# Attention by keys and values of each head in place of latent queries and outputs, with the work at three entries in another order

## What is computed

```
q = jnp.einsum('bsr,rhd->bshd', cq, w_uq)
q_lat = jnp.einsum('bshd,hdr->bshr', q, w_uk)
...
_, sel = lax.top_k(score, n_sel)                      # 64 keys per query
kv_sel = jax.vmap(lambda c, i: c[i])(ckv, sel)
att = jnp.einsum('bqhr,bqkr->bqhk', q_lat_b, kv_sel) * (A_HEAD_DIM ** -0.5)
att = att - slopes[None, None, :, None] * dist[:, :, None, :]
p = jax.nn.softmax(jnp.where(valid, att, -jnp.inf), axis=-1)
o_lat = jnp.einsum('bqhk,bqkr->bqhr', p, kv_sel)
return jnp.einsum('bqhr,hrd->bqhd', o_lat, w_uv)
...
return jnp.concatenate([o_a, o_b], axis=-1) @ w_out
```

## Time and profile before

| | us |
|---|---|
| median of 3 runs | 1978.47 |
| lowest and highest | 1975.74, 1982.19 |
| the profiled execution | 1978.86 |
| its span, first to last instruction | 1977.0 |
| TensorE busy | 1948.3 |
| VectorE, ScalarE, GpSimd busy | 1091.0, 845.2, 65.7 |
| mean granted TensorE clock, of full speed | 0.995 |

### The profile page before, as it was taken

One profiled execution on the slowest core, in us unless ns is written; L12 is line 12 of the kernel. 1 busy time (PEld: TensorE's weight loads), 2 busy tenths in 40 slices (PEclk: granted clock), 3 DMA queues, 4 the chain that ended last, 5 costly groups with the idle time before them and its releaser, 6 DMA issues.

```text
span 1977.0 us, 28705 instructions
## 1 busy us (share of the span) xinstructions
PE 1948.3 (99%) x10670; PEld 1661.4 (84%) x10670; DVE 1091.0 (55%) x1235; ACT 845.2 (43%) x944; POOL 65.7 (3%) x95
## 2 busy tenths in 40 slices
PE   9999999999999998999999999899999999999997
PEld 7888888888888887999999988788888888888886
DVE  5555545555445465677756757555545555544455
ACT  4444434444434343555645544344444444443332
POOL 0000000000000001300221100000000000000000
PEclk9999999999999999999999999999999999999999
DMA  8666665666566573755532057466666666556663
GB/s 293 190 189 190 191 182 179 190 200 210 190 204 203 193 244 95 223 180 148 142 98 87 22 186 261 131 189 190 189 182 183 193 197 190 186 169 194 208 197 144
DMA packets 185327, 357.30 MB, mean 181 GB/s; under 512 B 11296, under 2 KB 23584, under 8 KB 184240
## 3 DMA queue, kind: packets, MB, share of 16 engines
q1 hardware_dynamic: 183568, 347.43, 56.8%
q0 software_dynamic: 1696, 8.99, 1.4%
HBM read 354.28 MB, written 2.10 MB: 180 GB/s over the span
## 4 chain that ended last, share of the span: by engine, by line
PE 95%; DVE 3%; issue 1%; ACT 1%; DMA 0%; SPq 0%; POOL 0%; POOLq 0%; ACTq 0%; DVEq 0%
PE acc L370 27%; PE acc L372 27%; PE acc L371 27%; PE acc L393 3%; PE acc L397 3%; PE acc L395 3%; PE tp L727 1%; DVE wlo L358 1%; PE acc L1946 1%; PE tp L1959 0%; ACT whi L351 0%; PE acc L1972 0%; PE tp L448 0%; DMA raw<-in_ffn_w_gate_dram 0%; DVE work L1691 0%
## 5 line engine op out<-in xcount | busy, mean ns | idle before, releaser
L358 DVE TENSOR_TENSOR wlo<-raw,whi 128x1024 fp32r<-128x1024 f32 (+2 forms) x637 | 762.4, 1204 | 785.5 <-ACT whi L351 784.6
L351 ACT ACTIVATE whi<-raw 128x1024 fp32r<-128x1024 f32 (+2 forms) x637 | 656.2, 1039 | 943.4 <-PE acc L372 880.8
L370 PE MATMUL acc<-whi,xT 128*128 128x512 f32 (+2 forms) x1652 | 636.3, 385 | 13.6 <-DVE wlo L358 12.8
L372 PE MATMUL acc<-whi,xT 128*128 128x512 f32 (+2 forms) x1652 | 631.3, 382 | 0.0
L371 PE MATMUL acc<-wlo,xT 128*128 128x512 f32 (+2 forms) x1652 | 630.8, 382 | 0.0
L370 PEld LDWEIGHTS acc<-whi,xT 128*128 128x128 f32 x1652 | 311.6, 189 | 79.4 <-DVE wlo L358 12.8
L372 PEld LDWEIGHTS acc<-whi,xT 128*128 128x128 f32 x1652 | 311.6, 189 | 59.8
L371 PEld LDWEIGHTS acc<-wlo,xT 128*128 128x128 f32 x1652 | 311.8, 189 | 56.7
L370 PE MATMUL acc<-whi,hT 128*128 128x512 f32 x656 | 256.3, 391 | 0.0
L372 PE MATMUL acc<-whi,hT 128*128 128x512 f32 x656 | 255.4, 389 | 0.0
L371 PE MATMUL acc<-wlo,hT 128*128 128x512 f32 x656 | 255.4, 389 | 0.0
(11 more groups left out here) (299 smaller groups left out, 1283.7 us busy)
## 6 DMA issues: line engine op xcount, KB each, us to landing
raw<-in_ffn_w_up_dram SPq DMA_DIRECT2D x176, 512.0 KB, 3.7
raw<-in_ffn_w_down_dram SPq DMA_DIRECT2D x176, 512.0 KB, 4.6
raw<-in_ffn_w_gate_dram SPq DMA_DIRECT2D x175, 512.0 KB, 3.8
raw<-in_w_in_dram SPq DMA_DIRECT2D x48, 512.0 KB, 3.8
raw<-in_w_out_dram SPq DMA_DIRECT2D x32, 512.0 KB, 6.6
raw<-in_w_in_dram SPq DMA_DIRECT2D x32, 260.0 KB, 2.8
raw<-in_w_in_dram SPq DMA_DIRECT2D x16, 456.0 KB, 5.3
raw<-in_w_q_idx_dram SPq DMA_DIRECT2D x8, 512.0 KB, 4.2
```

What stands on the lines that cost most here:

```text
L351: act.activation(hi[:, s, :, 0:w], raw[:, r, :, 0:w], ACT.Copy).then_inc(hi_done, 1)
L358: dve.tensor_tensor(lo[:, s, :, 0:w], raw[:, r, :, 0:w], hi[:, s, :, 0:w].bitcast(F32), ALU.subtract).then_inc(lo_done, 1)
L370: pe.matmul(o, hi, w_hi[:, s, k, 0:width], start=first and k == 0, stop=False)
L372: ins = pe.matmul(o, lo, w_hi[:, s, k, 0:width], start=False, stop=last and k == UNIT_KT - 1)
```

## The change

The arithmetic of the attention is bracketed in another way. Before, `q_lat = q w_uk` was multiplied with the latents, and the probabilities with the latents and then with `w_uv`. Now `kT`, the keys of each head, is `w_uk` by the latents (per head 2 calls of 256 columns), and a logit is one product of `qT` and `kT`. `vatt`, the values of each head, is the latents by `w_uv` (8 calls of 512 columns for all heads), and a head's output is 3 calls of 128 columns. `w_uk` is laid out on the host with the latent first. `wuv` is loaded once the last score product is done (before: after `qlatT`), to another place. The logits of query tile 1 come first. ScalarE copies `vatt` around the first exponentials; copies, squares and sums of the delta rule stand elsewhere on ScalarE and VectorE; `nkcdT` stands behind the second part of the softmax; the two groups of transposes of L2142 now stand behind units 2 and 3 of the output projection.

At both entries the splits of units 9 and 10 stand ahead of the copies of (2, 1) and (3, 0), and the transposes of (3, 0) and (3, 1) on TensorE each stand one unit earlier. In the first chunk of feed-forward 1 gate and up units alternate for k = 0 and 1, and the later pieces of `x` are loaded behind units 1, 3, 5, 7.

The diff, without allocations and steps that only follow:

```diff
+        FIRST = [(0, 0), (1, 0), (0, 1), (1, 1)] + [(c, k) for c in range(2) for k in range(2, KU)]
+        FIRST_X = {1: 0, 3: 1, 5: 2, 7: 3}
...
             half_unit(7, 1)
+            tile_to_xT_pe(pe, e, 3, 0)
             for half in range(2):
                 half_unit(8, half)
-            tile_to_xT_pe(pe, e, 3, 0)
-            for half in range(2):
-                half_unit(9, half)
             tile_to_xT_pe(pe, e, 3, 1)
-            for v in range(10, 2 * KU):
+            for v in range(9, 2 * KU):
                 for half in range(2):
                     half_unit(v, half)
...
             split_hi(act, p, 0, 8)
+            split_hi(act, p, 0, 9)
             tile_to_xT_act(act, e, 2, 1)
+            split_hi(act, p, 0, 10)
             tile_to_xT_act(act, e, 3, 0)
-            split_hi(act, p, 0, 9)
             tile_to_xT_act(act, e, 3, 1)
-            split_hi(act, p, 0, 10)
...
             norm_tile(dve, e - 1, 3, 0)
             split_lo(dve, p, 0, 8)
-            tile_to_xT_dve(dve, e, 2, 1)
             norm_tile(dve, e - 1, 3, 1)
             split_lo(dve, p, 0, 9)
+            tile_to_xT_dve(dve, e, 2, 1)
+            split_lo(dve, p, 0, 10)
             tile_to_xT_dve(dve, e, 3, 0)
             tile_to_xT_dve(dve, e, 3, 1)
-            split_lo(dve, p, 0, 10)
...
+            for v, (c, k) in enumerate((FIRST, ENTRY)[f]):
+                if f == 0 and v == 0:
+                    load_first(sp, gate_v)
+                else:
                     load_unit(sp, GU[f], 0, v, (gate_v, up_v)[c][:, 2 * k:2 * k + 2, 0:BANK])
+                if f == 0 and v in FIRST_X:
+                    load_x(FIRST_X[v])
...
             pool.tensor_copy(ndist[:], ndist_i[:]).then_inc(sem("ndist"), 1)
+            pool.wait_ge(sem("score_ps"), SCORE_ITEMS)
+            pool.dma_start(wuv[:], w_uv[0].rearrange("h (t r) d -> r h t d", r=P)).then_inc(sem("wuv"), 16)
...
-            for h in range(AH):
-                act.wait_ge(sem("qlat_ps"), h + 1)
-                act.activation(qlatT[:, :, h, :], qlat_bank(h), ACT.Copy).then_inc(sem("qlat"), 1)
+            for pair in range(AH // 2):
+                act.wait_ge(sem("kT_ps"), pair + 1)
+                act.activation(kT[:, 2 * pair:2 * pair + 2, :], kT_bank(pair), ACT.Copy).then_inc(sem("kT"), 1)
             split_hi(act, WO, 0, LEAD)
...
+            def values(t):
+                act.wait_ge(sem("vatt_ps"), t + 1)
+                act.activation(vatt[:, t], all_heads((acc1, acc0)[t]), ACT.Copy).then_inc(sem("vatt"), 1)
+            values(0)
+            exps(0)
+            values(1)
             for b in range(2):
                 four("vnew0", b + 1, b, vnew0, acc1)
-            exps(0)
+            exps(1)
             for b in range(2):
                 four("state", b + 1, b, state, acc1)
-            exps(1)
             act.wait_ge(sem("o0_ps"), 1)
             act.activation(o_first[:], all_heads(acc0), ACT.Copy).then_inc(sem("o_out"), 1)
+            exps(2)
             for b in range(2):
                 four("vnew1", b + 1, b, vnew1, acc1)
-            exps(2)
+            act.wait_ge(sem("o_out"), 1)
+            act.activation(o_squares[:, 0], o_first[:], ACT.Square).then_inc(sem("o_sq"), 1)
             act.wait_ge(sem("pT_ps"), 1)
             act.activation(pT0[:, :, 0:P], tp[:, 0:2].rearrange("p b (h q) -> p (b h) q", h=4), ACT.Copy)\
...
+                oT_hi(h)
+                if h == 5:
                     act.wait_ge(sem("o_sum"), 2)
                     act.activation(o_squares[:, 1], o_second[:], ACT.Square).then_inc(sem("o_sq"), 1)
-            oT_hi(AH - 1)
...
             for q in range(2):
+                split_hi(act, WO, 0, 3 + q)
                 act.wait_ge(sem("yT_ps"), q + 1)
                 act.activation(xT[:, AH + 4 * q:AH + 4 * q + 4, 0, :], yT_banks(q), ACT.Copy)\
                    .then_inc(sem("y_hi"), 1)
...
             logits(1, range(AH // 2))
+            select(1)
+            logits(1, range(AH // 2, AH))
             for b in range(2):
                 dve.wait_ge(sem("nkcd_ps"), b + 1)
                 dve.tensor_scalar(nkcdT[:, 4 * b:4 * b + 4, :], heads4(acc0[:, b]), -1.0, None, ALU.mult)\
                    .then_inc(sem("nkcd"), 1)
-            select(1)
-            logits(1, range(AH // 2, AH))
             normalise(0)
...
             z_times_o(0, o_first[:])
+            o_mean_square(0)
             dve.wait_ge(sem("o_out"), 2)
...
                 dve.wait_ge(sem("pT_ps"), i + 1)
                 dve.tensor_copy(pT0[:, SOFTMAX[i][1], P:S], heads4(pT_bank(i, 0))).then_inc(sem(f"pT_part{i}"), 1)
+            for h in range(4):
+                oT_lo(h)
             dve.wait_ge(sem("o_out"), 3)
             dve.wait_ge(sem("o_sum"), 1)
             dve.tensor_tensor(o_second[:], o_second[:], o_state[:], ALU.add).then_inc(sem("o_sum"), 1)
-            o_mean_square(0)
-            oT_lo(0)
+            for h in range(4, AH):
+                oT_lo(h)
+            y_tile(0)
             dve.wait_ge(sem("o_sum"), 2)
-            oT_lo(1)
             o_mean_square(1)
-            oT_lo(2)
             dve.wait_ge(sem("o_sq"), 2)
             z_times_o(1, o_second[:])
-            oT_lo(3)
-            y_tile(0)
-            oT_lo(4)
             y_tile(1)
-            for h in range(5, AH):
-                oT_lo(h)
...
             for q in range(2):
+                split_lo(dve, WO, 0, 3 + q)
                 dve.wait_ge(sem("y_hi"), q + 1)
...
-            for h in range(AH):
-                if h < 4:
-                    pe.wait_ge(sem("relu"), SCORE_ITEMS - 3 + h)
-                else:
-                    pe.wait_ge(sem("qlat"), h - 3)
-                for r in range(RT):
-                    ins = pe.matmul(qlat_bank(h)[:, r, :], wuk[:, h, r * P:r * P + P], qT[:, h, :],
-                                    start=True, stop=True)
-                ins.then_inc(sem("qlat_ps"), 1)
-            for t in range(T):
+            for pair in range(AH // 2):
+                for j in range(2):
+                    for r in range(RT):
+                        ins = pe.matmul(kT_bank(pair)[:, j, :], wuk[:, r, 2 * pair + j, :], ckvT[:, r, :],
+                                        start=r == 0, stop=r == RT - 1)
+                ins.then_inc(sem("kT_ps"), 1)
+            pe.wait_ge(sem("relu"), SCORE_ITEMS)
+            for t in (1, 0):
                 n = (t + 1) * P
                 for h in range(AH):
-                    pe.wait_ge(sem("qlat"), h + 1 if t == 0 else AH)
-                    for r in range(RT):
-                        ins = pe.matmul((att_first, att_second)[t](h)[:, 0:n], qlatT[:, r, h, t * P:t * P + P],
-                                        ckvT[:, r, 0:n], start=r == 0, stop=r == RT - 1)
+                    pe.wait_ge(sem("kT"), h // 2 + 1)
+                    ins = pe.matmul((att_first, att_second)[t](h)[:, 0:n], qT[:, h, t * P:t * P + P], kT[:, h, 0:n],
+                                    start=True, stop=True)
                     if h % (4, 2)[t] == (3, 1)[t]:
                         ins.then_inc(sem("att_ps"), 1)
+            pe.wait_ge(sem("wuv"), 16)
+            for t in range(T):
+                if t == 1:
+                    pe.wait_ge(sem("att_z"), AH)
+                for b in range(2):
+                    for r in range(RT):
+                        ins = pe.matmul((acc1, acc0)[t][:, b], ckvT[:, r, t * P:t * P + P], wuv[:, 4 * b:4 * b + 4, r, :],
+                                        start=r == 0, stop=r == RT - 1)
+                ins.then_inc(sem("vatt_ps"), 1)
...
             pT_transposes(2)
-            pe.wait_ge(sem("pT_part1"), 2)
-            pe.wait_ge(sem("wuv"), 16)
-            def o_head(h):
-                pe.wait_ge(sem("olat"), h + 1)
-                if h == 0:
-                    pe.wait_ge(sem("o_out"), 2)
+            pe.wait_ge(sem("o_out"), 2)
+            for h in range(AH):
+                if h % 4 == 0:
+                    pe.wait_ge(sem(f"pT_part{h // 4 + 1}"), 2)
                 wait(pe, sem("oT_lo"), h - 3)
-                for r in range(RT):
-                    ins = pe.matmul(o_bank(h), wuv[:, h, r, :], olatT[:, r, h, :], start=r == 0, stop=r == RT - 1)
+                pe.matmul(o_bank(h)[:, 0:P], vatt[:, 0, h], pT0[:, h, 0:P], start=True, stop=True)
+                pe.matmul(o_bank(h)[:, P:S], vatt[:, 0, h], pT0[:, h, P:S], start=True, stop=False)
+                ins = pe.matmul(o_bank(h)[:, P:S], vatt[:, 1, h], pT1[:, h, :], start=False, stop=True)
                 ins.then_inc(sem("oT_ps"), 1)
...
-            pe.wait_ge(sem("o_out"), 3)
-            for h in range(AH):
...
-                    pe.matmul(bank[:, r, 0:P], ckv[:, 0, rc], pT0[:, h, 0:P], start=True, stop=True)
-                    pe.matmul(bank[:, r, P:S], ckv[:, 0, rc], pT0[:, h, P:S], start=True, stop=False)
-                    ins = pe.matmul(bank[:, r, P:S], ckv[:, 1, rc], pT1[:, h, :], start=False, stop=True)
```

(8 more changed lines are left out.)

105 lines of the change are left out of this document (40 added, 65 removed).

## The result

| | before | after |
|---|---|---|
| median, us | 1978.66 (4 runs) | 1951.19 (4 runs) |
| lowest and highest | 1975.74, 1982.19 | 1950.07, 1951.48 |
| the profiled execution | 1978.86 | 1951.33 |
| its span | 1977.0 | 1949.5 |
| ratio of the medians, 95% interval | | 0.9859, 0.9842 to 0.9876 |

What follows compares the result with a forecast made beforehand. It took TensorE's own products to bound the kernel, busy 1948.3 of 1977.0 us. Entries 18.2, start 0.7 and attention 9.5 summed to 28.4 us, taken from 1978.86: 1950.5 us, range 1946 to 1957.

Runs made afterwards that it cites:

- entries_only: The kernel before with only the entries' new order, on all three engines at both entries; attention and first chunk as before: 1961.64 us, ratio 0.9918.
- values_late_2: The kernel after, with `wuv` asked for only when the last `kT` is done, behind GpSimd's masking of the scores: 1952.77 us.
- values_late: The kernel after, with `wuv` asked for only when the last `kT` is done, ahead of GpSimd's masking of the scores: 1956.63 us.
- attention_only: The kernel before with all hunks of the change but those of the entries and the first chunk: 1971.07 us, ratio 0.9967.
- both_chains: The kernel after, with ScalarE's copies ahead of non-urgent exponentials, VectorE's `nkcdT` and transposed-probability copies earlier, splits of output projection units 3 to 5 earlier: 1947.61 us.

## What to carry to other kernels

Where in-order queues wait for one another in a ring, moving one link can be enough, as either did here; find the loop first, and then take the cheapest link. Where two engines' chains run side by side and meet, taking a wait off one of them tells nothing until the other has been followed up to the meeting point, every instruction of it; a wait that goes and turns up as two others on the same engine is the sign. And a DMA issued by an engine that also computes carries its wait into that engine's queue: put it behind the work that others are waiting for.

## What was new about the hardware

- The fall of TensorE's granted clock does not follow from the length of a wait. It fell behind 2.14 us (start of entries_only), 2.68 us (first entry of before), 2.19 and 2.21 us (values_late_2, values_late), 2.89 us in attention_only's unit 9, and 5.66 us. It did not fall behind 2.89 us in before's unit 9, with the same instructions around it, nor behind 3.54 us. What decides is open. Where the loss could be read, a fall cost 1.6 to 2.9 us.
- It may be what makes the time scatter. All executions of before lie between 1974.05 and 1982.19 us, on several chips, those of after and both_chains within 1.4 and 0.7 us. That such spells are the reason is argued from three profiles (before, attention_only, entries_only), not shown.
- A plain float32 call costs 0.223, 0.432 and 0.884 us for 128, 256 and 512 columns, in proportion to its columns within 4%, so larger calls save next to nothing per column here.
